# A two-block transformer on one core: a walk entry dropped, one added, denser row products in the down-projections, and the last half slab in two rounds

## What is computed

```python
def first_block(x, ...):                       # DEPTH = 1
    hn = rmsnorm(x, mix_norm_g)
    h = x + nsa_mixer(hn, rel_bias, nsa_w_in, nsa_w_out, ...)
    z = rmsnorm(h, ffn_norm_g) @ ffn_w_in      # D_FF = 5632
    h = h + (silu(z[..., :D_FF]) * z[..., D_FF:]) @ ffn_w_out
    return rmsnorm(h, final_norm_g)

def second_block(x, c, w_mod, b_mod, ...):
    mod = silu(c) @ w_mod + b_mod              # 2048 x 12288
    sh1, sc1, g1, sh2, sc2, g2 = split(mod, 6)
    h = rmsnorm(x, attn_norm_g) * (1.0 + sc1) + sh1
    x = x + g1 * (attention(h @ w_in) @ w_out)
    h = rmsnorm(x, mlp_norm_g) * (1.0 + sc2) + sh2
    u = relu(h @ w_ff1)
    x = x + g2 * ((u * u) @ w_ff2)             # D_FF_2 = 8192
    return rmsnorm(x, final_norm_g_2)
```

## Time and profile before

| what | before |
|---|---|
| time, median of 3 runs | 2122.11 us (2122.09 to 2123.37) |
| profiled execution | 2124.48 us, span 2122.7 us |
| granted TensorE clock, mean | 0.998 of full |
| PE busy | 99% of the span |
| DVE, ACT, POOL busy | 70%, 50%, 1% |
| loads, output | 496.16 MB by DMA, mean 234 GB/s |

### The profile page before, as it was taken

One profiled execution on the slowest core, in us unless ns is written; L12 is line 12 of the kernel. 1 busy time (PEld: TensorE's weight loads), 2 busy tenths in 40 slices (PEclk: granted clock), 3 DMA queues, 4 the chain that ended last, 5 costly groups with the idle time before them and its releaser, 6 DMA issues.

```text
span 2122.7 us, 29195 instructions
## 1 busy us (share of the span) xinstructions
PE 2101.6 (99%) x11412; PEld 1808.2 (85%) x11412; DVE 1485.0 (70%) x1985; ACT 1057.3 (50%) x1514; POOL 18.0 (1%) x32
## 2 busy tenths in 40 slices
PE   9999999999999999999999999999999999999998
PEld 7888888888888888888878898888888888888886
DVE  6867665889889787998956676576655565555655
ACT  7654555554444434444455665554443444344443
POOL 1000000000000000000000000000000000000000
PEclk9999999999999999999999999999999999999999
DMA  9785333789989998898955525455555555555553
GB/s 348 252 294 197 120 119 121 297 307 338 342 317 334 351 341 324 321 336 320 358 194 158 205 91 187 170 205 184 191 193 189 198 186 191 198 181 196 193 184 119
DMA packets 73064, 496.16 MB, mean 234 GB/s; under 512 B 8394, under 2 KB 8602, under 8 KB 16352
## 3 DMA queue, kind: packets, MB, share of 16 engines
q1 hardware_dynamic: 69840, 481.20, 62.8%
q0 software_dynamic: 2512, 12.44, 1.6%
q10 hardware_dynamic: 576, 0.66, 0.1%
HBM read 492.09 MB, written 2.16 MB: 233 GB/s over the span
## 4 chain that ended last, share of the span: by engine, by line
PE 93%; ACT 3%; DVE 2%; DMA 2%; issue 1%; SPq 0%; DVEq 0%; ACTq 0%
PE region L1032 40%; PE region L972 30%; PE region L976 15%; PE bank L1113 1%; PE bank L1070 1%; ACT m_WHI L1386 1%; DMA m_RAW<-in_nsa_w_in 1%; PE region L1021 1%; PE bank L1079 1%; PE bank L1011 1%; PE bank L1126 1%; DVE m_WLO L1742 0%; PE region L1022 0%; ACT m_HL L1574 0%; DMA m_RAW<-in_ffn_w_out 0%
## 5 line engine op out<-in xcount | busy, mean ns | idle before, releaser
L1742 DVE TENSOR_TENSOR m_WLO<-m_RAW,m_WHI 128x1024 fp32r<-128x1024 f32 (+3 forms) x729 | 870.0, 1206 | 511.0 <-ACT m_WHI L1386 490.4
L1386 ACT ACTIVATE m_WHI<-m_RAW 128x1024 fp32r<-128x1024 f32 (+3 forms) x729 | 754.0, 1045 | 701.6 <-PE region L1032 375.7
L1032 PE MATMUL region<-m_WHI,m_HL 128*128 128x512 f32 x1152 | 362.5, 396 | 0.6 <-DVE m_HL L1935 0.5
L972 PE MATMUL region<-m_HL,m_WHI 128*128 128x512 f32 x1472 | 357.8, 393 | 0.0
L972 PE MATMUL region<-m_H,m_WHI 128*128 128x512 f32 x1376 | 328.6, 391 | 0.0
L972 PEld LDWEIGHTS region<-m_HL,m_WHI 128*128 128x128 f32 x1472 | 269.4, 188 | 52.1 <-issue 0.3
L972 PEld LDWEIGHTS region<-m_H,m_WHI 128*128 128x128 f32 x1376 | 252.8, 188 | 48.9
L1032 PEld LDWEIGHTS region<-m_WHI,m_HL 128*128 128x128 f32 x1152 | 213.5, 189 | 43.7 <-issue 1.4
L1032 PE MATMUL region<-m_WLO,m_HL 128*128 128x512 f32 x576 | 225.3, 391 | 0.0
L1778 DVE CUSTOM_DVE_ANT_0 m_RAW<-m_RAW,m_CROW,m_consts 128x2048 f32<-128x2048 f32 x96 | 225.1, 2345 | 0.0
L1032 PE MATMUL region<-m_WHI,m_HIDH 128*128 128x512 f32 x512 | 199.2, 389 | 0.0
(11 more groups left out here) (314 smaller groups left out, 1729.2 us busy)
## 6 DMA issues: line engine op xcount, KB each, us to landing
m_RAW<-in_w_ff SPq DMA_DIRECT2D x124, 1024.0 KB, 4.9
m_RAW<-in_w_mod SPq DMA_DIRECT2D x96, 1024.0 KB, 6.5
m_RAW<-in_ffn_w_in SPq DMA_DIRECT2D x88, 1024.0 KB, 6.5
m_RAW<-in_ffn_w_out SPq DMA_DIRECT2D x44, 1024.0 KB, 6.6
m_RAW<-in_nsa_w_in SPq DMA_DIRECT2D x36, 1024.0 KB, 5.5
m_RAW<-in_nsa_w_out SPq DMA_DIRECT2D x16, 1024.0 KB, 4.9
m_RAW<-in_w_out SPq DMA_DIRECT2D x16, 1024.0 KB, 5.0
m_RAW<-in_w_in SPq DMA_DIRECT2D x8, 1024.0 KB, 6.7
```

Of the source, the lines that this page charges most:

```text
L972: mm = e.matmul(region[s["reg"]][:, b, :], hi[:, i, c:c + 128], both[:, k + a + i, :, :].rearrange("p a s -> p (a s)"), start=k + a + i == ...
L1032: mm = e.matmul(o, lhs, rhs, start=start and i == 0, stop=fin and i == 2, skip_group_check=True)
L1386: e.activation(WHI[u % 4][:, 0:(z - a) * ncol], raw[:, a * ncol:z * ncol], ACT.Copy).then_inc(a_hi, 1)
L1742: e.tensor_tensor(WLO[u % 4][:, 0:m], raw[:, a * ncol:z * ncol], WHI[u % 4][:, 0:m].bitcast(F32), ALU.subtract).then_inc(v_lo, 1)
```

## The change

Four edits. The first empty run of `every` has 7 places instead of 8, so that everything behind it comes a chunk sooner. Behind head 0's s2 stands one more empty place in `side`. The row products' rate goes from 0.75 to 1.0 in out1's last two slabs and in the down-projections, and stays 0.75 in the up-projections. In the last slab the second row half is multiplied in two rounds of 256 columns, the first into the slab's own region, the second into bank 7, with a `tail` entry behind each; the sums of squares get a fifth place, and the second row half leaves in pieces of 256, 512, 512, 256 and 512 columns, in five transfers instead of four.

```diff
@@ finish_by_halves
+        if which is None:
+            for n, kk in st["held"]:
+                put("mmq", n, kk, 0)
+            put("tail", 0)
+            P.uses(("mmtail",), 7)
+            for n, kk in st["held"]:
+                put("mmq", n, kk, 1)
+            put("tail", 1)
+            st["held"].clear()
+            put("stat4", 1)
+            put("store", 1)
+            return
@@ make_plan
-    every.extend([None] * 8)
+    every.extend([None] * 7)
     every.append(lambda: side.extend([None] * 4 + [("rowsq",), ("stat", 0)] + [None] * 4 + [("rowcast", 0), ("makez", 0), ("toep",), None, None, ("zsplit", 0)]))
@@ attention
             side.append(s2)
+            if at + i == 0:
+                side.append(None)
@@ make_plan
     st["rate"] = 1.3
-    st["gemv"] = 0.75
+    st["gemv"] = 1.0
     run(out1[2], out1[3])
     for up, dn in ffn1:
+        st["gemv"] = 0.75
         run(*up)
+        st["gemv"] = 1.0
         side.extend([None] * 8 + [("warm", 0)])
         run(*dn)
@@ tensor engine, weights(n, kk, half=0, quarter=None)
+                if quarter is not None:
+                    c, width = c + 256 * quarter, 256
                 o = region[s["reg"]][:, b, off:off + width]
+                if quarter == 1:
+                    o, start = bank[7][:, 0:256], (n, kk) == tail_first
+                    if start:
+                        bank_empty(("mmtail",), 7)
@@ scalar engine
+            elif name == "tail":
+                q, = arg
...
+                w.wait_ge(a_sumsq, 39 + q)
+                c = 1536 + 256 * q
+                e.activation(JUNK3[:, 0:256], X[:, 1, c:c + 256], ACT.Square, accum_out=sums[:, 3, 1, 3 + q:4 + q]).then_inc(a_sumsq, 1)
@@ vector engine
+            elif name == "tail":
+                q, = arg
+                c = slice(1536 + 256 * q, 1792 + 256 * q)
+                wide, own = (slice(1536, 2048), slice(0, 512)) if q == 0 else (c, slice(0, 256))
+                sums_of = region[name_slab("down2z", 12)["reg"]][:, 1, :] if q == 0 else bank[7][:, 0:256]
...
+                e.tensor_tensor(GATED[:, 1, own], sums_of, GROW[:, wide], ALU.mult).then_inc(v_gmul, 1)
...
+                e.tensor_tensor(X[:, 1, wide], GATED[:, 1, own], X[:, 1, wide], ALU.add).then_inc(v_x if q else v_xtail, 1)
...
+                e.tensor_tensor(YROW[:, 1, c], X[:, 1, c], GROW2[:, c], ALU.mult).then_inc(v_yg if q else v_ytail, 1)
@@ store
-                for m0 in (0, 4, 8):
-                    y = YROW[:, h, 128 * m0:128 * m0 + 512]
-                    w.wait_ge(v_yg, m0 // 2 + h + 1)
+                for a, z in ((0, 512), (512, 1024), (1024, 1536)) if h == 0 else ((0, 256), (256, 768), (768, 1280), (1280, 1536)):
+                    y = YROW[:, h, a:z]
+                    w.wait_ge(v_yg, 2 * ((z - 1) // 512) + h + 1)
                     e.tensor_scalar(y, y, rstdc[:, h:h + 1], None, ALU.mult).then_inc(v_store, 1)
```

More of the change, by code:

```diff
@@ L392, in finish_by_halves @@
         row_half(s, 1)
-        if which is None:
-            put("stat4", 1)
-            put("store", 1)
-            return
         idle(5)
@@ L979, in half_of_part, with weights @@
                 mm.then_inc(p_part, 1)
-        def weights(n, kk, half=0):
+        def weights(n, kk, half=0, quarter=None):
             s, k, nk, last = CHUNKS[n]
@@ L1032, in weights @@
                     mm = e.matmul(o, lhs, rhs, start=start and i == 0, stop=fin and i == 2, skip_group_check=True)
-            if by_halves and half == 0:
+            if by_halves and half == 0 or quarter == 0:
                 if fin:
@@ L1146, in tensor_program @@
                 weights(*arg, half=1)
+            elif name == "mmq":
+                n, kk, q = arg
+                tail_first = tail_first or (n, kk)
+                weights(n, kk, half=1, quarter=q)
             elif name == "xturn":
@@ L1971, in vector_program @@
                 if r == 2:
-                    step(e.tensor_reduce(total[:, :, :], sums[:, 0:2, :, :], AX_X, ALU.add))
+                    step(e.tensor_reduce(total[:, :, :], sums[:, 0:2, :, 0:4], AX_X, ALU.add))
                     stepped()
@@ L1977, in vector_program @@
                 elif r > 0:
-                    ins = e.tensor_reduce(total[:, 0, :], sums[:, stage, :, :], AX_X, ALU.add)
+                    ins = e.tensor_reduce(total[:, 0, :], sums[:, stage, :, 0:4], AX_X, ALU.add)
                 if r > 0:
```

59 lines of the change are left out of this document (44 added, 15 removed).

## The result

The changed kernel takes 2131.08 us in the median of 5 runs (2127.33 to 2133.27), the kernel before 2122.11 in as many (2122.03 to 2123.37); the ratio is 1.0036, with a 95% interval of 1.0025 to 1.0047. It is slower by some 8 us. I had forecast 2121.7 us, and a range that ended at 2125.6.

What follows compares the result with a forecast made beforehand. PE was taken as the bound, busy 2101.6 of 2122.7 us. The terms +2.1 + 1.8 - 3.7 + 0 - 0.5 gave -0.3, with rounding -0.4, so 2122.11 became 2121.7 us, range 2116.0 to 2125.6.

Steps and rivals of the forecast that it cites:

- The first norm, +2.1: Sum for moving the first norm's entries a chunk sooner: 1.0 - 0.6 + 1.7 = +2.1 us.
- the longer wait: Before `rowcast` at the first norm, PE waits 2.36 us instead of 1.25 and loses about 1.0 us.
- the wait for ZHL: At the first norm, PE's wait of 0.58 us for ZHL goes because PE itself is late: -0.6 us.
- The third, +1.7 for low halves: Behind the first norm, splits that Z and ZHL moved ahead of come late: 0.95, 0.55 and 0.2 us, +1.7.
- The rival of the falling clock: At the first norm, the clock falls after PE's longer wait: +1.7 us, in all 2123.4; chance 0.11.
- The empty place, +1.8: Behind the first head: -0.7 us before head 2's scores, +2.45 for three later waits, sum +1.8.
- The denser row products, -3.7 and 0: Row products at 1.0: -3.7 us at the first slab of `down1z`, 0 in `down1`.
- -2.04 - 1.7 = -3.7: At `down1z`'s first slab, PE's 2.04 us wait for XG and 1.7 us from the clock's fall both go.
- I take 0 for it: In `down1`, one row product per chunk asks 385 GB/s; the leads hide the lack, so no cost.
- The prediction's own sign of being wrong: In `down1`, PE's waits for splits summing to more than 1 us would show the prediction wrong.
- the queue can't carry one to one: Rival in `down1`: under 358 GB/s, loads decide; at 350 GB/s +8 us, in all 2129.7; chance 0.09.
- The last slab, -0.5: Two rounds at the end: +0.25 us of matmuls, -0.9 behind the last one, +0.1 on DVE; sum -0.5.

Runs made afterwards that it cites:

- e1: Kernel before with only the first norm's entries a chunk sooner (7 empty places instead of 8): 2124.80 us, ratio 1.0013.
- e2: As e1, with PE also multiplying 16 small idle tiles into bank 7 in the wait before `rowcast`: 2125.14 us, ratio 1.0010.
- e9: The kernel before, unchanged, profiled once more: 2121.30 us.
- e8: Kernel before with row products at an even 0.8 in out1's last two slabs, the up- and the down-projections: 2124.21 us, ratio 1.0010.
- e6: As e4, but each load of a row product brings only its first half, 512 KB instead of 1 MB: 2124.29 us, ratio 1.0007.
- e10: Kernel before with the last slab's two rounds and down1z's turning matmuls two places later, row products at 0.75: 2120.13 us, ratio 0.9988.
- e13: e10 with the row products at 1.0 as in the change: 2124.06 us, ratio 1.0009.
- e4: Kernel before with only the denser row products (1.0 in out1's last two slabs and the down-projections): 2126.43 us, ratio 1.0014.

## Why the prediction was wrong

**The first norm, +2.1.** About right: e1 gives +2.2 by the medians and +2.8 by the ratio. Of its terms the longer wait is confirmed, 2.07 us against 2.36, with rstd at 50.02 against 50.3, and the wait for ZHL went (-0.6). The third, +1.7 for low halves, is seen only in e2, as 1.3; in the profiled executions of e1 and of the change nothing of it is left, and the lower clock stands in its place. So that the sum came out is in part luck. The rival of the falling clock, which I had as another case with +1.7, is not another case but a part of the executions, and its price goes by how long the fall lasts: 10 us of it made +4.9 of the place in the changed kernel's profiled one, 3.4 us made +2.5 in e1's, no more than e2 has without a fall. The wait before `rowcast` itself differs between executions of one order (1.25 us in the rows above, 1.52 in e9, 1.97 in e8, 2.47 in e6); that an order which adds 0.8 to it meets the fall more often is likely, and not shown.

**The empty place, +1.8.** Right: +2.1 by the parts, +2.3 by the ratio, with the three waits (0.49, 0.74, 0.90) where 0.55, 1.05 and 1.0 were written.

**The denser row products, -3.7 and 0.** This is where it failed, in both its steps. "*-2.04 - 1.7 = -3.7*" took the price of a stall from one execution and subtracted it from a median; e9 shows 0.33 us and no fall of the clock at that place, seven profiles 1.4 us in the middle, and e10 and e13 that a typical execution has 1 to 2 us to give there. The sign that it was so stood in the prediction: the profiled execution was 2.4 us above its median, and no step asked where. "*I take 0 for it*" in `down1` let 385 GB/s be asked of a queue that had shown 360 to 380, and hid the lack behind ACT's leads. The queue shows 369 to 386 by the execution; in e4 and the changed kernel the leads were used up after 8 and 14 chunks, by the first slips at 733 and 766 us in a phase that begins near 690. PE was idle for 0.7 to 1.8 us where it waited, 1.7 to 2.8 by the parts (the modelled ends of matmuls count as busy and hide part of a wait). The prediction's own sign of being wrong, more than 1 us of waits for splits in `down1`, came true with 1.8. The rival *the queue can't carry one to one* was the right mechanism, put at 0.09 and priced with 350 GB/s. The Trainium skill (DMA: Bandwidth & Descriptors, Where 436 GB/s comes from) has some 358 GB/s for a core between HBM and SBUF, by which the prediction itself had reckoned 5 us in `down1` and then left them out; the number is not this case's, for the windows of `down1` lie above it, up to 386. And the row products added in out1 were counted and not placed: where they are at 1.0, a chunk of ffn_w_in comes late behind out1 and costs 0.9 to 2.9 us. In the sum, a gain of 1 to 2 us and a price of some 4 (3.9 by e13 over e10) replace -3.7 and 0.

**The last slab, -0.5.** Measured -0.3 by the medians, -0.7 by the parts; within what was written, and too small for its ratio, so its sign isn't shown.

With the measured terms the sum is 2.8 + 2.3 + 3.0 - 0.4 = +7.7 us by the four ratios, 2129.8; the change has +7.6 by its own, a closer match than ratios known to 2 us apiece could promise.
